# First turn of a two-layer mixer kernel: the order of its loads, and conditioning chunks taken in pairs

## The chip, the cores and the metric

The kernel runs on one core of one Trainium2 chip. The metric is the device time of one execution in microseconds; the time before is the median of 3 executions. The profile is of one execution, and its times count from the first instruction.

## The reference, cut to what matters

Two layers, each with D = 2048, a sequence of S = 256, and float32 data:

```python
mod = silu(c) @ w_ada + b_ada                 # w_ada: 2048 x 6144, one row of c
shift, scale, gate = split(mod, 3)
h = rmsnorm(x, norm_pre) * (1 + scale) + shift
z = h @ w_in                                  # w_in: 2048 x 14336, split into conv and retention parts
...                                           # short convolution, retention, group norm, gates
o = concat(y_conv, y_ret) @ w_out             # 4096 x 2048
x = x + gate * rmsnorm(o, norm_post)
```

The first layer's `h` needs the scale and the shift of every one of its 2048 rows of K, and for these all of `w_ada`'s first 4096 columns: 32 MB, before the last row group of `h` can be multiplied.

## The kernel before

**Units of work.** A weight chunk `n` is 512 columns of `w_in` or `w_out` by 2 or 4 tiles of K (0.5 or 1 MB). ScalarE rounds it (`cast`, line 586, w_hi), VectorE takes the rest (`low`, line 798, w_lo), and TensorE forms three products for each K tile and each of the two token tiles (`products`, lines 1247 to 1249): 12 matmuls for a chunk of 2 tiles, 24 for one of 4.

**The first turn** (chunks 0 to 34) goes by five K groups of 2, 2, 4, 4 and 4 tiles (`FRONT_GROUPS`), and in each group over the same seven column blocks, so that work can begin before all of the conditioning is there. Group g's chunks are 7g to 7g+6. Chunks 0 to 13 are 0.5 MB, later ones 1 MB. The sum of a block over the groups is kept in SBUF (`part`): VectorE adds chunk m's product to it (line 998) behind `low(m+2, 0)`, and TensorE waits for that add before it starts chunk m+2, which uses the same bank of PSUM (`z_wait`).

**Conditioning.** For each group there are two rows, k = 2g (scale) and k = 2g+1 (shift), each made of 2 or 4 conditioning chunks (k, kc) of 1 MB of `w_ada`, 32 in all. A chunk is taken either by TensorE (`front_chunk`, line 1286, 8 or 16 small matmuls in a 128x32 tiling into bank A) or by VectorE (`front_rows`, lines 940 and 943). Which, is said by `FRONT_VECTOR`. When all chunks of row k are in, VectorE brings bank A to SBUF (`front_row`), TensorE transposes it (`front_sum`, line 1299), VectorE reduces it and adds the bias (`front_mods`, lines 831 to 840), ScalarE forms h and rounds it (`h_full`, lines 601 and 607), and VectorE splits it (`front_split`, line 853). Only then may the group's first chunk be multiplied.

**Order.** Every engine works its queue in order, and the orders are written out by hand as tables over n: `FRONT_ROW` and `FRONT_SUM` say after which chunk a row is brought over and transposed, `FRONT_MOD` in which chunk's work VectorE forms its mods. `h_full` of group g stands on ScalarE at the end of chunk 7g-1, ahead of `cast(7g, 0)`; for group 2 (`FRONT_LATE`, chunk 14) it stands behind `cast(14, 0)`, with `front_split` behind `low(14, 0)` on VectorE. One queue (SyncE's) issues all large loads, in the order of `load_table`. There are two rings of 4 slots each, one for weight chunks and one for conditioning chunks, and SyncE waits in order for the slot of each load: that of weight chunk n-4 is free when its `low` is done, that of a conditioning chunk when TensorE or VectorE has taken it.

Of the kernel before, what the change touches and what calls it, by code (L numbers as in the profile page):

```python
# [14 lines left out]
ACT = mybir.ActivationFunctionType  # L15
# [6 lines left out]
NT = S // P  # L22
# [24 lines left out]
BLOCKS = 7  # L47
# [9 lines left out]
FRONT_GROUPS = ((0, 2), (2, 2), (4, 4), (8, 4), (12, 4))  # L57
# [7 lines left out]
def chunk_table():  # L65
# [7 lines left out]
    for l in range(LAYERS):  # L73
# [5 lines left out]
        for nb in range(NB):  # L79
            for w in range(OUT_CH):  # L80
# [8 lines left out]
FRONT = len(FRONT_GROUPS) * BLOCKS  # L89
# [25 lines left out]

FRONT_AFTER = [1, 1, 1, 1, 1, 1, 1] + [2, 1, 1, 1, 1, 1, 1] + [2, 1, 1, 1, 1, 1, 1] + [2, 1, 1, 1, 0, 0, 0]
FRONT_AFTER += [0] * BLOCKS
FRONT_CHUNKS = [(2 * g + part, kc) for g, (_, tiles) in enumerate(FRONT_GROUPS) for part in range(2)  # L120
                for kc in range(tiles)]
FRONT_FIRST = 2 * FRONT_GROUPS[0][1]
FRONT_BLOCKS = 2 * len(FRONT_GROUPS)


FRONT_VECTOR = {0: (), 1: (), 2: (), 3: (), 4: (1, 3), 5: (1,), 6: (3,)}

FRONT_LATE = 2 * BLOCKS
FRONT_ROW = {2: 2, 4: 3, 8: 4, 11: 5, 15: 6, 18: 7, 22: 8, 25: 9}
FRONT_SUM = {2: 2, 4: 3, 8: 4, 11: 5, 16: 6, 18: 7, 23: 8, 25: 9}
FRONT_MOD = {3: 2, 6: 3, 10: 4, 13: 5, 18: 6, 20: 7, 25: 8, 27: 9}

# [29 lines left out]
GATE_CHUNKS, GATE_SUM, GATE_AT = (0, 2, 4, 5), 6, 7  # L167


def front_after(n):  # L170

    at = FRONT_FIRST + sum(FRONT_AFTER[:n])
    return FRONT_CHUNKS[at:at + FRONT_AFTER[n]] if n < FRONT else []


def on_vector(k, kc):
    return kc in FRONT_VECTOR.get(k, (1, 3))


def front_done(k, kc):  # L180
# [10 lines left out]
def load_table():  # L191


    table = [("front", k, kc) for k, kc in FRONT_CHUNKS[:FRONT_FIRST]]
    for n, c in enumerate(CH):
        for m, at in enumerate(ADA_CHUNKS):
            if n in at:
                table.append(("ada", m, at.index(n)))
        if c.out and c.g in GATE_CHUNKS:
            table.append(("gate", NB * c.l + c.j, GATE_CHUNKS.index(c.g)))  # L200
        table.append(("w", n, 0))
        table += [("front", k, kc) for k, kc in front_after(n)]
    return table


# [19 lines left out]
def build(nc, x, c, positions, norm_pre, norm_post, w_ada, b_ada, w_in, conv_w, gn_gain, w_out,  # L225
          consts, decay, out):
    ctx = ExitStack()
    with ctx:  # L228
# [21 lines left out]
        xt = sb("xt", [P, NT, D])  # L250
# [24 lines left out]
        xsq = sb("xsq", [P, NT, 2])  # L275
# [10 lines left out]
        rows, _ = place("rows", [P, 2, D], F32, at_h)  # L286
        og, _ = place("og", [P, NT, D], F32, at_h + 4 * 2 * D)
        part, _ = place("part", [P, BLOCKS, NT, BLK], F32, at_yc)
        next_hi, _ = place("next_hi", [P, 2, 2, BLK], F32R, at_yr)
        next_lo, _ = place("next_lo", [P, 2, 2, BLK], F32R, at_yr + 4 * 4 * BLK)  # L290
# [287 lines left out]
        def _(act):  # L578
            N = nc.scalar

            def cast(n, h):
                if h == 0:
                    act.wait_ge(s_stage[slot_of(n)], STAGED["w", n, 0])
                if w_free(n, h):
                    act.wait_ge(s_pe, w_free(n, h))
                N.copy(w_bufs(n, h)[0], stage[:, slot_of(n), 2 * h:2 * h + 2, :]).then_inc(s_hi, 1)  # L586
# [23 lines left out]
            def h_full(l, k0, tiles):  # L610
                for k in range(k0, k0 + tiles, 2):
                    h_unit(l, k // 4, k % 4 // 2, None)

            def x_scaled(g):

                if g == 0:
                    act.wait_ge(s_pow, 1)
                else:
                    act.wait_ge(s_xt, COLUMN[0, g - 1, None] + 1)
                k0, tiles = FRONT_GROUPS[g]  # L620
                for i in range(NT):
                    ins = N.activation(v_sb[:, i, 0:P * tiles], xt[:, i, P * k0:P * (k0 + tiles)], ACT.Copy,
                                       scale=rs2[:, NT + i:NT + i + 1])
                ins.then_inc(s_xs, 1)
# [35 lines left out]
            for i in range(NT):  # L660
                act.dma_start(pos_i[:, i:i + 1], positions[0, i * P:(i + 1) * P].rearrange("(p o) -> p o", o=1))\
                    .then_inc(s_pos, 16)

            act.wait_ge(s_prm, 2)
            act.wait_ge(s_ones, 2)
            N.activation(c_cols[:, :, 0], prm[:, PRM_C:PRM_C + KT], ACT.Silu).then_inc(s_cs, 1)
            N.activation(c_silu[:, :], prm[:, PRM_C:PRM_C + KT], ACT.Silu).then_inc(s_cs, 1)
            act.wait_ge(s_x, 32)
            for i in range(NT):
                N.activation(part[:, 2 * i:2 * i + 2, :, :].rearrange("p a b c -> p (a b c)"), xt[:, i, :], ACT.Square,  # L670
                             accum_out=xsq[:, i, 0:1]).then_inc(s_xsq, 1)

            x_scaled(0)
            h_full(0, *FRONT_GROUPS[0])
            for n, ch in enumerate(CH):
                cast(n, 0)
                if n - SPILL < BLOCKS and n >= SPILL:

                    m = n - SPILL
# [111 lines left out]
        def _(dve):  # L791
# [3 lines left out]
            def low(n, h):  # L795
                hi, lo = w_bufs(n, h)
                dve.wait_ge(s_hi, HALVES[n] + h + 1)
                V.tensor_tensor(lo, stage[:, slot_of(n), 2 * h:2 * h + 2, :], hi.bitcast(F32), ALU.subtract)\  # L798
                    .then_inc(s_lo, 1)
# [44 lines left out]
            def h_split(l, g, half, i=None):  # L844
                k, lo = unit_tiles(half), tokens(i)
                tmp = tmp_buf(g)[:, k.start:k.stop, lo]
                k, hi = slice(4 * g + k.start, 4 * g + k.stop), slice(S + lo.start, S + lo.stop)
                unit = UNIT[l, g, half, i]
                if l:
                    dve.wait_ge(s_tmp, unit + 1)  # L850
                    V.tensor_copy(H[:, k, lo], tmp).then_inc(s_hhi, 1)
                dve.wait_ge(s_hhi, unit + 1)
                V.tensor_tensor(H[:, k, hi], tmp, H[:, k, lo].bitcast(F32), ALU.subtract).then_inc(s_h, 1)
# [74 lines left out]
            def front_rows(k, kc):  # L928

                tile, sem_, value = front_tile(k, kc)  # L930
                at, rows_ = front_rows_of(k, kc)
                sums = front_acc(k)[:, 0:P * FRONT_GROUPS[k // 2][1]]
                dve.wait_ge(sem_, value)
                first = min(FRONT_VECTOR.get(k, (1, 3)))
                if kc == first:
                    dve.wait_ge(s_sum, k - 1)
                for a in range(rows_):
                    c_a = c_silu[:, at + a:at + a + 1]
                    if (kc, a) == (first, 0):
                        ins = V.tensor_scalar(sums, tile[:, a, :], c_a, None, ALU.mult)  # L940
                    else:
                        me.wait()
                        ins = V.scalar_tensor_tensor(sums, tile[:, a, :], c_a, sums, ALU.mult, ALU.add)
                    me.then(ins)
                me.wait()
                dve.sem_inc(s_fv, 1)

            def front_row(k):

                cols = slice(0, P * FRONT_GROUPS[k // 2][1])  # L950
                dve.wait_ge(s_front, front_done(k, front_last(k)))
                if not FRONT_VECTOR.get(k, True):
                    if k > 1:
                        dve.wait_ge(s_sum, k - 1)
                    V.tensor_copy(front_acc(k)[:, cols], A[:, k % 2, cols]).then_inc(s_row, 1)
                else:
                    V.tensor_tensor(front_acc(k)[:, cols], A[:, k % 2, cols], front_acc(k)[:, cols], ALU.add)\
                        .then_inc(s_row, 1)

            def front_mods(k):  # L960
                mods(k, 0, 1 - k % 2, *FRONT_GROUPS[k // 2], A[:, k % 2, :])
                if k % 2:
                    gains(0, *FRONT_GROUPS[k // 2], k + 1)

            def front_split(g):
                k0, tiles = FRONT_GROUPS[g]
                for k in range(k0, k0 + tiles, 2):
                    h_split(0, k // 4, k % 4 // 2)
# [10 lines left out]
            front_mods(0)  # L979
            front_row(1)  # L980
            front_mods(1)
            h_split(0, 0, 0)

            ada_seen = 0
            for n, ch in enumerate(CH):
                low(n, 0)
                for m in range(BLOCKS, FRONT):
                    if n != m + SPILL:
                        continue
# [7 lines left out]
                    dst = v_sb[:, :, :] if (was.g, was.b) == (LAST_GROUP, VV) else part[:, was.b, :, :]  # L997
                    V.tensor_tensor(dst, Z[m % 2][:, :, :], part[:, was.b, :, :], ALU.add).then_inc(s_fin, 1)
                if n == FRONT_LATE:
                    front_split(ch.g)  # L1000
                if n == NEXT + 1:
                    x_end(0)
# [11 lines left out]
                if n == NEXT + 1:  # L1014
# [5 lines left out]
                    diagonal(1)  # L1020
                    for g in range(2):
                        h_split(1, g, None, 1)
                if n in FRONT_MOD:
                    front_mods(FRONT_MOD[n])
                if n in FRONT_ROW:
                    front_row(FRONT_ROW[n])
                if n < FRONT and ch.g < LAST_GROUP:
                    if ch.b == BLOCKS - 1 and n + 1 != FRONT_LATE:
                        front_split(ch.g + 1)
                for k, kc in front_after(n):  # L1030
                    if on_vector(k, kc):
                        front_rows(k, kc)
                if ch.l == 1 and not ch.out and ch.j == 0 and ch.b == QK and ch.g > 1:
# [183 lines left out]
        def _(pe):  # L1217
# [126 lines left out]
            for n, ch in enumerate(CH):  # L1344
# [11 lines left out]
                if n not in chain(*BY_TILES):  # L1356
                    z_wait(n)
                    for h in range(ch.halves):
# [6 lines left out]
                        pe.wait_ge(s_lo, HALVES[n] + h + 1)  # L1365
                        for i in range(NT):
                            products(n, h, i)
                for k, kc in front_after(n):
                    if not on_vector(k, kc):
                        front_chunk(k, kc)  # L1370
                if n < FRONT and ch.g < LAST_GROUP:
# [112 lines left out]
```

## Time and profile before

| | |
|---|---|
| time, median of 3 (lowest to highest) | 1730.48 us (1729.69 to 1733.38) |
| span of the profiled execution | 1727.3 us |
| TensorE busy, share of the span | 1686.8 us, 98% |
| weight loads, VectorE, ScalarE busy | 80%, 67%, 42% |
| read from HBM | 417.57 MB, mean 243 GB/s |
| mean rate in the first 200 us | 337 GB/s |

The page gives no time for the profiled execution beside its span; the median lies 3.2 us above that. Lengths of matmuls are modelled and overlap, so the starts are what counts. In rows, "idle before" is the time in which the engine stood still ahead of the instruction, with what released it.

### The profile page before, as it was taken

How to read it: one execution, taken by the hardware profiler on the slowest of the kernel's cores; microseconds unless marked ns; L12 is line 12 of the kernel's file. 1: busy time of each engine (PE TensorE's matmuls, PEld its weight loads, DVE VectorE, ACT ScalarE, POOL GpSimd, SP SyncE). 2: the span in 40 equal slices, each digit the busy share in tenths (PEclk: the TensorE clock that was granted, in tenths of full speed). 3: DMA queues.
4: the chain of work that ended last, by engine and by line, in shares of the span. 5: the costliest groups of instructions: out<-in, count | busy, mean ns of one | idle time of the engine just before them, and what ended most of it. 6: DMA issues, size and time to landing. Idle time of an engine off the chain costs nothing. (4 is left out here: it accounts for less than half of the span.)

```text
span 1727.3 us, 18931 instructions
## 1 busy us (share of the span) xinstructions
PE 1686.8 (98%) x7715; PEld 1375.8 (80%) x7715; DVE 1151.9 (67%) x1279; ACT 717.3 (42%) x800; POOL 52.5 (3%) x94
## 2 busy tenths in 40 slices
PE   6899999999999999999999999999999999999998
PEld 3567888888878887888878888888888888888886
DVE  2788767778677777777776456556555654577776
ACT  3344444434343443443454444444434444443432
POOL 4000000000000000000000000000000000000000
PEclk9999999999999999999999999999999999999999
DMA  9998665797788778877774665566556656668775
GB/s 342 383 381 317 210 202 194 258 304 264 248 290 286 276 251 296 318 273 278 280 250 164 197 202 196 189 197 219 192 179 201 216 188 189 209 243 301 284 281 190
DMA packets 233655, 429.25 MB, mean 249 GB/s; under 512 B 8664, under 2 KB 50024, under 8 KB 232800
## 3 DMA queue, kind: packets, MB, share of 16 engines
q1 hardware_dynamic: 225888, 408.97, 68.6%
q10 hardware_dynamic: 7680, 19.07, 4.1%
q8 instruction: 61, 1.00, 0.2%
q14 instruction: 26, 0.21, 0.0%
HBM read 417.57 MB, written 2.10 MB: 243 GB/s over the span
## 5 line engine op out<-in xcount | busy, mean ns | idle before, releaser
L798 DVE TENSOR_TENSOR w_lo<-stage,w_hi 128x1024 fp32r<-128x1024 f32 x574 | 692.2, 1223 | 488.6 <-ACT w_hi L586 486.3
L586 ACT CAST w_hi<-stage 128x1024 fp32r<-128x1024 f32 x574 | 594.7, 1051 | 950.8 <-PE Z L1249 559.9
L1247 PE MATMUL Z<-w_hi,H 128*128 128x512 f32 x1784 | 702.7, 394 | 15.3 <-DVE w_lo L798 9.9
L1249 PE MATMUL Z<-w_hi,H 128*128 128x512 f32 x1784 | 695.1, 390 | 0.0
L1248 PE MATMUL Z<-w_lo,H 128*128 128x512 f32 x1784 | 694.4, 389 | 0.0
L1247 PEld LDWEIGHTS Z<-w_hi,H 128*128 128x128 f32 x1784 | 335.0, 188 | 95.0 <-issue 13.3
L1249 PEld LDWEIGHTS Z<-w_hi,H 128*128 128x128 f32 x1784 | 334.9, 188 | 70.7
L1248 PEld LDWEIGHTS Z<-w_lo,H 128*128 128x128 f32 x1784 | 335.2, 188 | 67.6
L819 DVE SCALAR_TENSOR_TENSOR acc<-stage,c_silu,acc 128x512 f32<-128x512 f32 x240 | 180.2, 751 | 6.8
L1247 PE MATMUL Z<-w_hi,YC 128*128 128x512 f32 x256 | 102.0, 399 | 0.0
L1247 PE MATMUL Z<-w_hi,YR 128*128 128x512 f32 x256 | 100.6, 393 | 0.0
L1249 PE MATMUL Z<-w_hi,YC 128*128 128x512 f32 x256 | 99.7, 390 | 0.0
L1249 PE MATMUL Z<-w_hi,YR 128*128 128x512 f32 x256 | 99.7, 389 | 0.0
L1248 PE MATMUL Z<-w_lo,YC 128*128 128x512 f32 x256 | 99.7, 389 | 0.0
L1248 PE MATMUL Z<-w_lo,YR 128*128 128x512 f32 x256 | 99.6, 389 | 0.0
L1248 PEld LDWEIGHTS Z<-w_lo,YC 128*128 128x128 f32 x256 | 48.1, 188 | 11.3 <-issue 1.4
L1247 PEld LDWEIGHTS Z<-w_hi,YC 128*128 128x128 f32 x256 | 48.1, 188 | 11.3 <-issue 1.4
L1247 PEld LDWEIGHTS Z<-w_hi,YR 128*128 128x128 f32 x256 | 48.1, 188 | 10.7 <-DVE w_lo L798 0.6
L1248 PEld LDWEIGHTS Z<-w_lo,YR 128*128 128x128 f32 x256 | 48.1, 188 | 10.2 <-issue 0.2
L1249 PEld LDWEIGHTS Z<-w_hi,YR 128*128 128x128 f32 x256 | 48.1, 188 | 10.1
L1249 PEld LDWEIGHTS Z<-w_hi,YC 128*128 128x128 f32 x256 | 48.0, 188 | 10.0
L1188 POOL MEMSET behind<- 1x512 f32 (+1 forms) x16 | 7.9, 517 | 966.2 <-DVE mv L1093 886.3
(152 smaller groups left out, 727.5 us busy)
## 6 DMA issues: line engine op xcount, KB each, us to landing
stage<-in_w_in SPq DMA_DIRECT2D x186, 1024.0 KB, 5.3
stage<-in_w_ada SPq DMA_DIRECT2D x64, 1024.0 KB, 7.4
stage<-in_w_out SPq DMA_DIRECT2D x64, 1024.0 KB, 7.4
stage<-in_w_in SPq DMA_DIRECT2D x74, 512.0 KB, 5.3
front_stage<-in_w_ada SPq DMA_DIRECT2D x32, 1024.0 KB, 11.9
behind<-R ACTq DMA_DIRECT2D x14, 448.0 KB, 3.6
taps<-in_conv_w ACTq DMA_DIRECT2D x18, 256.0 KB, 6.6
xt<-in_x SPq DMA_DIRECT2D x2, 1024.0 KB, 6.7
```

The source lines that it names most:

```text
L586: N.copy(w_bufs(n, h)[0], stage[:, slot_of(n), 2 * h:2 * h + 2, :]).then_inc(s_hi, 1)
L798: V.tensor_tensor(lo, stage[:, slot_of(n), 2 * h:2 * h + 2, :], hi.bitcast(F32), ALU.subtract)\
L819: ins = V.scalar_tensor_tensor(acc[:, :], w, c_silu[:, k:k + 1], acc[:, :], ALU.mult, ALU.add)
L1188: ins = G.memset(behind_buf(t)[0:n_back, n_back - 1, 0, :], 0.0)
L1247: T.matmul(z[:, i, :], hh, wh, start=ch.first and a == 0, stop=False)
L1248: T.matmul(z[:, i, :], hh, wl, start=False, stop=False)
L1249: ins = T.matmul(z[:, i, :], hl, wh, start=False, stop=stop)
```

## The change

Loads: the weight chunks of a group go ahead, and conditioning chunks follow in pairs. Use: the place at which an engine takes a conditioning chunk (`FRONT_USE`) is now apart from the place of its load, and TensorE takes two chunks, one behind the other, after every second weight chunk or so. VectorE keeps one chunk (kc = 1) of each of the rows 6 to 9 and gives up the other six. The places of `FRONT_ROW`, `FRONT_SUM` and `FRONT_MOD` move with that. At the start, ScalarE's two squares of x come ahead of its two Silus, `cast(0, 0)` ahead of `h_full` of group 0, and VectorE's `low(0, 0)` ahead of its `h_split`. In chunk 14, `front_mods(5)` stands right ahead of `front_split`, where it stood in chunk 13.

```diff
-FRONT_AFTER = [1, 1, 1, 1, 1, 1, 1] + [2, 1, 1, 1, 1, 1, 1] + [2, 1, 1, 1, 1, 1, 1] + [2, 1, 1, 1, 0, 0, 0]
-FRONT_AFTER += [0] * BLOCKS
-FRONT_CHUNKS = [(2 * g + part, kc) for g, (_, tiles) in enumerate(FRONT_GROUPS) for part in range(2)
-                for kc in range(tiles)]
+FRONT_CHUNKS = [(2 * g + part, kc) for g in range(3) for part in range(2) for kc in range(FRONT_GROUPS[g][1])]
+FRONT_CHUNKS += [(2 * g + part, kc) for g in (3, 4) for part, kc in ((0, 0), (0, 2), (0, 1), (0, 3), (1, 0), (1, 1), (1, 2), (1, 3))]
...
-FRONT_VECTOR = {0: (), 1: (), 2: (), 3: (), 4: (1, 3), 5: (1,), 6: (3,)}
+FRONT_VECTOR = {k: (1,) if k >= 6 else () for k in range(2 * len(FRONT_GROUPS))}
...
+FRONT_LOAD = {2: 2, 4: 2, 7: 2, 9: 2, 11: 2, 12: 2, 15: 2, 16: 2, 17: 2, 18: 2, 22: 2, 23: 2, 24: 2, 25: 2}
...
+FRONT_USE = {1: ((2, 0), (2, 1)), 3: ((3, 0), (3, 1)), 6: ((4, 0), (4, 1)), 8: ((4, 2), (4, 3)),
+             10: ((5, 0), (5, 1)), 12: ((5, 2), (5, 3))}
+for g in (3, 4):
+    FRONT_USE[BLOCKS * g - 7] = ((2 * g, 0), (2 * g, 2))
+    FRONT_USE[BLOCKS * g - 5] = ((2 * g, 1), (2 * g, 3), (2 * g + 1, 0))
+    FRONT_USE[BLOCKS * g - 3] = ((2 * g + 1, 1), (2 * g + 1, 2), (2 * g + 1, 3))
 
 FRONT_LATE = 2 * BLOCKS
-FRONT_ROW = {2: 2, 4: 3, 8: 4, 11: 5, 15: 6, 18: 7, 22: 8, 25: 9}
-FRONT_SUM = {2: 2, 4: 3, 8: 4, 11: 5, 16: 6, 18: 7, 23: 8, 25: 9}
-FRONT_MOD = {3: 2, 6: 3, 10: 4, 13: 5, 18: 6, 20: 7, 25: 8, 27: 9}
+FRONT_ROW = {2: 2, 4: 3, 9: 4, 13: 5, 17: 6, 19: 7, 24: 8, 26: 9}
+FRONT_SUM = FRONT_ROW
+FRONT_MOD = {3: 2, 5: 3, 10: 4, 14: 5, 18: 6, 20: 7, 25: 8, 27: 9}
...
+            act.wait_ge(s_x, 32)
+            for i in range(NT):
+                N.activation(part[:, 2 * i:2 * i + 2, :, :].rearrange("p a b c -> p (a b c)"), xt[:, i, :], ACT.Square,
+                             accum_out=xsq[:, i, 0:1]).then_inc(s_xsq, 1)
             act.wait_ge(s_prm, 2)
...
             x_scaled(0)
+            cast(0, 0)
             h_full(0, *FRONT_GROUPS[0])
             for n, ch in enumerate(CH):
-                cast(n, 0)
+                if n:
+                    cast(n, 0)
...
             front_mods(1)
+            low(0, 0)
             h_split(0, 0, 0)
...
                 if n == FRONT_LATE:
+                    front_mods(FRONT_MOD[n])
                     front_split(ch.g)
...
-                for k, kc in front_after(n):
+                for k, kc in FRONT_USE.get(n, ()):
                     if on_vector(k, kc):
                         front_rows(k, kc)
```

TensorE's loop gets the same `FRONT_USE`, and `load_table` takes `front_loaded(n)`, which reads `FRONT_LOAD`. `on_vector` and `front_row` look `FRONT_VECTOR` up without a default.

## Rows read from the trace of the kernel before

**Rows 1.** The page: busy time of each engine, share of the span.

```profile
PE 1686.8 (98%) x7715; PEld 1375.8 (80%) x7715; DVE 1151.9 (67%) x1279; ACT 717.3 (42%) x800; POOL 52.5 (3%) x94
```

**Rows 2.** Windows by stage, whole core.

```profile
core 0: us, PE busy (x) PEld busy (x) DVE busy (x) ACT busy (x) POOL busy (x), PEclk, DMA share, GB/s
28.50:52.30 23.80, 23.71 (x152) 15.64 (x152) 10.53 (x13) 9.71 (x11) 8.93 (x15) 1.00 1.07 374
...
98.00:114.00 16.00, 14.43 (x73) 10.54 (x75) 15.57 (x17) 5.15 (x6) 0.00 (x0) 1.00 1.05 387
...
131.00:160.00 29.00, 29.00 (x144) 21.38 (x143) 25.29 (x31) 14.63 (x18) 0.00 (x0) 1.00 1.02 371
```

**Rows 3.** Waits of TensorE from 28 to 170 us: total, times, longest.

```profile
PE Z L1247 <- DVE w_lo L798: 6.0, 5, 1.8
PE Z L1247 <- DVE part L998: 3.0, 3, 1.4
PE Z L1247 <- DVE H L853: 2.2, 1, 2.2
```

**Rows 4.** Timeline, ScalarE: casts that waited for a load (chunks 2, 5, 13).

```profile
31.81 1.05 ACT L586 CAST w_hi<-stage 128x1024 fp32r<-128x1024 f32 x1 [2.92 <-DMA stage<-in_w_in]
...
46.81 1.05 ACT L586 CAST w_hi<-stage 128x1024 fp32r<-128x1024 f32 x1 [2.78 <-DMA stage<-in_w_in]
...
82.08 1.05 ACT L586 CAST w_hi<-stage 128x1024 fp32r<-128x1024 f32 x1 [2.98 <-DMA stage<-in_w_in]
```

**Rows 5.** Timeline, all engines: from row 9's transposes to chunk 28.

```profile
170.91 0.60 PE L1299 MATMUL A<-ident,acc 128*128 128x128 f32 x4
...
173.38 0.68 DVE L831 TENSOR_REDUCE c_sum<-A 128x4 f32<-128x512 f32 x1
...
174.49 1.02 ACT L601 ACTIVATE R<-B,mod,ga 128x256 f32<-128x256 f32 x2 [2.33 <-DVE ga L840]
...
177.64 1.99 ACT L586 CAST w_hi<-stage 128x1024 fp32r<-128x1024 f32 x2
...
179.86 1.22 DVE L998 TENSOR_TENSOR part<-Z,part 128x1024 f32<-128x1024 f32 x1
...
182.27 0.39 PE L1247 MATMUL Z<-w_hi,H 128*128 128x512 f32 x1
```

**Rows 6.** Timeline, TensorE: single conditioning chunks between products.

```profile
72.66 0.39 PE L1249 MATMUL Z<-w_hi,H 128*128 128x512 f32 x1
...
73.97 0.50 PE L1247 MATMUL Z<-w_hi,H 128*128 128x512 f32 x1
...
89.16 1.06 PE L1286 MATMUL A<-front_stage,c_cols 128*32 128x512 f32 x8
...
89.62 0.61 PE L1286 MATMUL A<-front_stage,c_cols 128*32 128x512 f32 x4
```

**Rows 7.** Timeline, TensorE: start and last product of chunks 24 and 25.

```profile
159.89 0.47 PE L1247 MATMUL Z<-w_hi,H 128*128 128x512 f32 x1
...
170.67 0.39 PE L1249 MATMUL Z<-w_hi,H 128*128 128x512 f32 x1
...
171.26 0.48 PE L1247 MATMUL Z<-w_hi,H 128*128 128x512 f32 x1
```

**Rows 8.** Timeline, TensorE and ScalarE: how chunk 14 started.

```profile
89.99 1.00 ACT L601 ACTIVATE R<-B,mod,ga 128x256 f32<-128x256 f32 x2
...
92.47 0.47 PE L1247 MATMUL Z<-w_hi,H 128*128 128x512 f32 x1 [2.24 <-DVE H L853]
```

**Rows 9.** Groups by line, 28.5 to 170 us: VectorE's conditioning chunks.

```profile
L943 DVE SCALAR_TENSOR_TENSOR acc<-front_stage,c_silu,acc 128x512 f32<-128x512 f32 x34 | 25.5, 751 | 1.1
```

**Rows 10.** Timelines at the start: ScalarE, VectorE, TensorE.

```profile
7.27 1.28 ACT L666 ACT_TABLE_LOAD   x1 [7.27 <-issue]
...
27.18 1.23 DVE L798 TENSOR_TENSOR w_lo<-stage,w_hi 128x1024 fp32r<-128x1024 f32 x1 [0.26 <-ACT w_hi L586]
...
28.55 0.47 PE L1247 MATMUL Z<-w_hi,H 128*128 128x512 f32 x1 [1.46 <-DVE w_lo L798]
```

More of the change, by code:

```diff
@@ L167, with front_loaded @@
 GATE_CHUNKS, GATE_SUM, GATE_AT = (0, 2, 4, 5), 6, 7
-def front_after(n):
-    at = FRONT_FIRST + sum(FRONT_AFTER[:n])
-    return FRONT_CHUNKS[at:at + FRONT_AFTER[n]] if n < FRONT else []
+def front_loaded(n):
+    at = FRONT_FIRST + sum(count for m, count in FRONT_LOAD.items() if m < n)
+    return FRONT_CHUNKS[at:at + FRONT_LOAD.get(n, 0)]
 def on_vector(k, kc):
-    return kc in FRONT_VECTOR.get(k, (1, 3))
+    return kc in FRONT_VECTOR[k]
 def front_done(k, kc):
@@ L201, in load_table @@
         table.append(("w", n, 0))
-        table += [("front", k, kc) for k, kc in front_after(n)]
+        table += [("front", k, kc) for k, kc in front_loaded(n)]
     return table
@@ L667, in _ @@
             N.activation(c_silu[:, :], prm[:, PRM_C:PRM_C + KT], ACT.Silu).then_inc(s_cs, 1)
[L668 to L671, printed above, removed]
             x_scaled(0)
+            cast(0, 0)
             h_full(0, *FRONT_GROUPS[0])
             for n, ch in enumerate(CH):
-                cast(n, 0)
+                if n:
+                    cast(n, 0)
                 if n - SPILL < BLOCKS and n >= SPILL:
@@ L933, in front_rows @@
                 dve.wait_ge(sem_, value)
-                first = min(FRONT_VECTOR.get(k, (1, 3)))
+                first = min(FRONT_VECTOR[k])
                 if kc == first:
@@ L951, in front_row @@
                 dve.wait_ge(s_front, front_done(k, front_last(k)))
-                if not FRONT_VECTOR.get(k, True):
+                if not FRONT_VECTOR[k]:
                     if k > 1:
@@ L985, in _ @@
             for n, ch in enumerate(CH):
-                low(n, 0)
+                if n:
+                    low(n, 0)
                 for m in range(BLOCKS, FRONT):
@@ L1022, in _ @@
                         h_split(1, g, None, 1)
-                if n in FRONT_MOD:
+                if n in FRONT_MOD and n != FRONT_LATE:
                     front_mods(FRONT_MOD[n])
@@ L1367, in _ @@
                             products(n, h, i)
-                for k, kc in front_after(n):
+                for k, kc in FRONT_USE.get(n, ()):
                     if not on_vector(k, kc):
```

## The prediction

> **What bounds the kernel now.** I read the page first: TensorE is busy for 98% of the span [rows 1], so the end moves only by what TensorE waits or works more or less. The windows then split the first turn. Up to 114 us the loads run at 374 to 387 GB/s, a DMA share over 1, and TensorE has gaps; from 114 us it has none, while VectorE is nearly full to 131 us and busy 25.3 of the 29.0 us after that [rows 2]. TensorE's granted clock is 1.00 in all of these stages [rows 2]. The waits say what the gaps are: 11.2 us in nine waits [rows 3], of which 1.46 us stand ahead of the first product, at 28.55 us [rows 10], so 9.7 us lie later. The largest, 2.2 us, is for h of group 2, ahead of chunk 14 [rows 3, 8]. All that this change can win is in these waits; whatever it adds to TensorE's queue behind them costs its full length. I take the kernel in two pieces, up to chunk 14 and from there to chunk 28. Behind chunk 28 nothing changes, and TensorE's lead or lag is carried to the end.
>
> **Loads up to chunk 14.** 1 MB at 387 GB/s takes 2.71 us. Before `cast(13)`, which had to wait for its data until 82.08 us [rows 4], 27.25 MB were asked for: x 2, conditioning 18, weights 7, decay 0.25. In the new order there are 16 conditioning chunks ahead of chunk 13: 25.25 MB, so it lands at 82.08 - 2 x 2.71 = 76.7 us. I checked SyncE's queue for new stalls: (5,0) needs the slot of (4,0), taken behind chunk 6 at about 54 us, when 3 MB are still under way; (6,0) needs that of (5,0), free at about 71 us, with 4 MB under way. The stream does not run dry.
>
> From `cast(13, 0)` to the end of the add behind `low(13, 0)` it is 3.44 us by the same sequence at chunk 28 (cast at 177.64, add ending at 179.86 + 1.22 = 181.08) [rows 5]. That gives 80.1 us, and chunk 13 starts at 80.2. TensorE could be there at 77.8: (3,1) is 12.75 MB into the stream, which between chunk 2 (9.5 MB, 31.81 us) and chunk 5 (14.25 MB, 46.81 us) [rows 4] is 42.1 us; then come 1.1 us for that chunk, nine products of 2.75 us (a matmul each 0.2294 us, 47 steps in 10.78 us [rows 7]), four pairs at 2.08 (below) and an estimated 1.5 us of transposes. So a shift of up to 2.3 us in the earlier work changes nothing. In this slack lie all edits of the start. `low(0, 0)` ahead of `h_split` can bring the first product forward by at most 28.55 - 27.18 = 1.4 us [rows 10]. A second activation table load between Square and Silu, of which the trace has only one, hidden, 1.28 us long [rows 10], would delay the first conditioning by about that. I take both as nothing, 0 to 0.5 us if they should meet other slips.
>
> Chunk 13 takes 2.85 us: row 5's transposes start at 83.0. From the start of such transposes to VectorE's reduce it is 0.63 us (0.60 and a hand-over), from the reduce to ScalarE's first activation 174.49 - 173.38 = 1.11 us [rows 5], from there to the product 92.47 - 89.99 = 2.48 us [rows 8]. Sum: **chunk 14 starts at 87.2 us, 5.3 us ahead** of its 92.47.
>
> **Work from chunk 14 to 28.** Before, 182.27 - 92.47 = 89.8 us [rows 5, 8]. What changes:
>
> Waits that go: of the 3.0 us for VectorE's adds [rows 3], the two behind chunk 14 hold 1.6 us. They came of `front_rows` standing in VectorE's queue; VectorE loses six conditioning chunks of four operations of 0.75 us [rows 9], 18 us of queue, and from 114 us on this was not on TensorE's path. -1.6.
>
> Conditioning on TensorE: six single chunks become six pairs. A single one costs from the last product's start, 72.66, to the next product, 73.97, 1.31 us in place of a step of 0.23, and 0.11 more because the first step behind it is longer: 1.19 us [rows 6]. Its second round of four matmuls starts 0.46 us behind the first (89.62 against 89.16) [rows 6], so a second chunk adds about two rounds, 0.89 us, and a pair costs 2.08; the bound above is 2 x 1.19 = 2.38, the one below 4 x 0.43 + 0.1 = 1.84. I take 2.08, as the row shows 0.3 us at the ends that a pair pays once. +6 x 2.08 - 6 x 1.19 = +5.3 (bounds +3.9 and +7.1).
>
> A rule bears on this. The row has 0.3 us per change between the 128x32 and the 128x128 tiling [rows 6]. The Trainium skill, page "TensorEngine Tiling (Array Packing)", section "Tiling Modes", says that changing the mode drains TensorE, and changing only the tile does not. By it a pair saves one of two drains, as I took it; without it the sum would be 1.8 us higher.
>
> New waits at chunks 21 and 28. This is the step that speaks against the change. Row 7's transposes stood behind chunk 18 and row 9's behind chunk 25, each with two products of 5.5 us ahead of the group that needs them. Now they stand behind chunks 19 and 26: one product is left, 0.35 us of transposes (171.26 - 170.91) plus 5.51 us [rows 7], 5.86 us of cover. The chain that must fit under it: 0.63 us to the reduce, then 181.08 - 173.38 = 7.70 us [rows 5] through mods, gains, two h units of two tiles each on ScalarE, `cast` of the group's first chunk (which stands behind `h_full` in ScalarE's queue), `low`, and the add ahead of that bank's use; 0.06 us to the product. That is 8.39 us, so TensorE stands still for 2.5 us, twice. Before, the reduce came 1.8 us later than the transposes allowed, and the chain still fitted. VectorE and ScalarE have nothing else in that stretch: their casts are released by products two half-chunks back. +5.1.
>
> Loads here: (7,0) needs the slot of (6,0), taken only behind chunk 14, and the stream may run dry for 1 to 2 us; but chunk 19's weights are needed 5 us after they would land, and (9,3) is needed 8 us after. 0.
>
> Sum: 89.8 - 1.6 + 5.3 + 5.1 = 98.6 us, so chunk 28 starts at 87.2 + 98.6 = 185.8, **3.5 us behind** its 182.27. A span of 1727.3 + 3.5 = 1730.8 us, and with the median lying 3.2 us above the profiled span, 1734.0 us.
>
> **Rivals.**
> 1. Chunk 13's data come earlier (no loss): the place is the stream's order up to 76.7 us, the price 1 us for each, up to the 2.3 us at which TensorE itself is the limit. Against it, `cast(13)` waited for its data with every queue full. Already 0.1 us decides that the loss stays under 0.2%; in full, +1.2 us: 1731.7.
> 2. The chain at chunks 21 and 28 is covered: it would have to be 5.86 us long in place of 8.39. Nothing in the rows shortens it; 3.5 - 5.1 = -1.6: 1728.9.
> 3. A pair costs two full chunks (2.38): +1.8, so +5.3: 1735.8. For it: no pair of 512-column chunks stands in the trace.
> 4. SyncE, waiting for a conditioning slot, holds back weights, and chunk 14 starts 2 to 3 us later: 1736.5. For it: pairs free their slots in bursts. Against: 3 to 4 MB under way.
> 5. Rivals 1 and 2 together, with the start's 1.4 us showing: -5: 1725.5.
>
> **How the numbers follow.** About 0.2%, 3.5 us, is what a measurement of this kernel can tell from no change. My forecast, +2.9 to +5, has 0.42, and a fifth of that is under the bound; rival 1 has 0.22, rival 2 0.10, rival 3 0.12, rival 4 0.08, rival 5 0.06. Slower: 0.34 + 0.12 + 0.08 = 0.54; same: 0.08 + 0.22 + 0.10 = 0.40; faster: 0.06. The likeliest case alone gives 1733.4 to 1735.5. The range must reach from half of rival 2 to rival 4: 1730.0 to 1737.0.
>
> **What would show it.** Right: the waits of TensorE up to 80 us sum to 3 to 5 us instead of nearly 10; chunk 13 waits for an add; chunk 14 starts at 87 us; pairs from start to next product take 2.1 to 2.2 us; two new waits of 2.5 us for VectorE's line 998 or 798 at about 134 and 183 us; chunk 28 starts at 186 us. Wrong: chunks 21 and 28 start without a wait, or chunk 14 starts above 89 or below 86 us, or waits come up behind chunk 28, which I hold to be shifted as a whole.

## The result, and the profile after

The changed kernel takes 1737.34 us (median of 6, 1734.82 to 1741.97) against 1728.99 us for the kernel before in the same comparison (6 runs): a ratio of 1.0044, 95% interval 1.0034 to 1.0053, or 7.6 us slower (the two medians alone lie 8.35 us apart). I had forecast slower with a chance of 0.54, and 3.5 us. The direction was right, and the 3.5 us were half of what came. The median lies just above my range of 1730 to 1737; 1728.99 us times the ratio, 1736.6, lies just inside it.

The page of the changed kernel (span 1733.8 us), against [rows 1]:

```profile
PE 1695.2 (98%) x7763; PEld 1382.4 (80%) x7763; DVE 1135.7 (66%) x1255; ACT 718.4 (41%) x801; POOL 51.8 (3%) x94
```

The waits of TensorE from 28 to 170 us (total, times, longest), which answer to [rows 3]; line 1011 is the add that was line 998, and the "issue" is the wait for h of group 2, ahead of chunk 14:

```profile
PE Z L1261 <- DVE part L1011: 4.2, 2, 2.3
PE Z L1261 <- issue: 3.7, 1, 3.7
PE A L1300 <- DMA front_stage<-in_w_ada: 0.8, 1, 0.8
```

And those from 170 to 200 us, where the kernel before had none:

```profile
PE Z L1261 <- DVE part L1011: 2.3, 1, 2.3
```

So waits up to 170 us fell from 11.2 to 8.7 us; without the 1.46 us ahead of the first product, which now starts at 26.87 us and ahead of this window, from 9.7 to 8.7. A new one of 2.34 us stands at chunk 28 as one does at chunk 21. The waits at chunks 13, 21 and 28 are those that I forecast, and the 3.65 us ahead of chunk 14 are in my sum for its start, though I did not name them. Up to 80 us they are 0.84 and 1.85, 2.7 us, a little under the 3 to 5 that I gave as a sign. What I did not forecast is in the windows by stage (PEclk is the granted clock, a mean over the window):

```profile
core 0: us, PE busy (x) PEld busy (x) DVE busy (x) ACT busy (x) POOL busy (x), PEclk, DMA share, GB/s
...
80.00:84.50 4.50, 4.48 (x13) 3.52 (x14) 2.92 (x3) 1.81 (x3) 0.00 (x0) 0.62 1.05 387
88.00:94.50 6.50, 5.78 (x14) 4.57 (x15) 4.97 (x6) 4.90 (x9) 0.79 (x2) 0.50 1.05 387
...
130.00:150.00 20.00, 17.66 (x87) 12.91 (x86) 14.79 (x18) 10.31 (x14) 0.00 (x0) 1.00 0.82 291
189.00:198.00 9.00, 8.71 (x31) 7.07 (x32) 7.32 (x8) 2.78 (x3) 0.00 (x0) 0.81 0.71 227
```

TensorE's clock was 1.00, 2.4 GHz, in all the stages of [rows 2]. Here it was granted 0.62 of it from 80 to 84.5 us, 0.50 (1.2 GHz) from 88 to 94.5 and 0.81 from 189 to 198. The timeline of TensorE in these places:

```profile
76.24 1.06 PE L1300 MATMUL A<-front_stage,c_cols 128*32 128x512 f32 x8
...
80.02 0.50 PE L1261 MATMUL Z<-w_hi,H 128*128 128x512 f32 x1 [1.85 <-DVE part L1011]
...
84.18 0.44 PE L1263 MATMUL Z<-w_hi,H 128*128 128x512 f32 x1
84.46 0.60 PE L1313 MATMUL A<-ident,acc 128*128 128x128 f32 x4
88.72 0.77 PE L1261 MATMUL Z<-w_hi,H 128*128 128x512 f32 x1 [3.65 <-issue]
...
96.77 0.39 PE L1263 MATMUL Z<-w_hi,H 128*128 128x512 f32 x1
97.09 1.92 PE L1300 MATMUL A<-front_stage,c_cols 128*32 128x512 f32 x16
98.94 0.50 PE L1261 MATMUL Z<-w_hi,H 128*128 128x512 f32 x1
...
189.29 0.50 PE L1261 MATMUL Z<-w_hi,H 128*128 128x512 f32 x1 [2.34 <-DVE part L1011]
```

Chunk 13, 12 products, starts at 80.02 us as forecast (80.2), but its last product starts 4.16 us later and not 2.6. Chunk 14 starts at 88.72; its 24 products take 8.05 us from the first start to the last, where 6.1 are usual for this chunk (6.08 in the kernel before). A pair takes 98.94 - 96.77 = 2.17 us from the last product to the next, against 1.31 for a single chunk [rows 6]. Chunk 28 starts at 189.29 us, 7.0 us behind [rows 5]; at 1.2 GHz for a part of it, it and the next four take 28.7 us where 27.1 are usual. With its first transposes for the retention heads (`turned`, at 209.47 us in the kernel before) the changed kernel is 8.77 us behind. I use the lag at this place to compare the runs below. It is read from one execution of each, and it is not carried whole to the end: in the changed kernel it has shrunk to 6.5 us at the end of the span. Between 430 and 970 us TensorE's waits for `low` (line 798, now 809) came to 3.9 us in the profile before, 2.1 in this one and 5.4 in that of e3 below, so a lag and a ratio can differ by 2 us.

The chain ahead of chunk 28, in all engines' timeline, answers to [rows 5]:

```profile
180.88 0.60 PE L1313 MATMUL A<-ident,acc 128*128 128x128 f32 x4
181.52 0.69 DVE L842 TENSOR_REDUCE c_sum<-A 128x4 f32<-128x512 f32 x1 [2.03 <-PE A L1313]
...
182.64 1.02 ACT L610 ACTIVATE R<-B,mod,ga 128x256 f32<-128x256 f32 x2 [8.07 <-DVE ga L851]
...
185.79 3.88 ACT L595 CAST w_hi<-stage 128x1024 fp32r<-128x1024 f32 x4
...
188.02 1.22 DVE L1011 TENSOR_TENSOR part<-Z,part 128x1024 f32<-128x1024 f32 x1
```

From transposes to product it is 189.29 - 180.88 = 8.41 us. I had 8.39.

At the start, the timeline of ScalarE shows a second table load between the squares and the Silus:

```profile
12.79 0.19 ACT L675 ACTIVATION_READ_ACCUMULATOR part<-xt 128x1 f32 x1
13.00 1.28 ACT L679 ACT_TABLE_LOAD   x1
14.29 0.23 ACT L679 ACTIVATE c_cols<-prm 128x16 f32<-128x16 f32 x1
```

### The profile page after: what moved, and what is told of

The parts are those of the page before. It is cut to its first block and busy times, and to the rows that moved or that the text cites. A ratio compares the mean times of both kernels' runs of the same rounds, so it can differ in the third digit from the quotient of the medians.

```text
span 1733.8 us, 18994 instructions
## 1 busy us (share of the span) xinstructions
PE 1695.2 (98%) x7763; PEld 1382.4 (80%) x7763; DVE 1135.7 (66%) x1255; ACT 718.4 (41%) x801; POOL 51.8 (3%) x94
## 5 line engine op out<-in xcount | busy, mean ns | idle before, releaser
L1261 PEld LDWEIGHTS Z<-w_hi,H 128*128 128x128 f32 x1784 | 336.2, 188 | 91.3 <-issue 11.1
```

What stands on the lines that cost most here:

```text
L1261: T.matmul(z[:, i, :], hh, wh, start=ch.first and a == 0, stop=False)
```

## The experiments

Ratios are to the kernel before, in one comparison each, with the 95% interval. "Lag" is that of the first transposes for the retention heads behind 209.47 us, in the profile.

| kernel | ratio | lag, us |
|---|---|---|
| the change | 1.0044 (1.0034 to 1.0053) | +8.8 |
| e1_sums_earlier | 0.9996 (0.9987 to 1.0006) | +0.1 |
| e2_casts_ahead | 0.9995 (0.9986 to 1.0005) | -1.0 |
| e3_late_sums_alone | 1.0036 (1.0022 to 1.0050) | +4.5 |
| e4_filled_waits | 1.0014 (1.0005 to 1.0023) | +3.4 |
| e5_silu_first | 1.0036 (1.0023 to 1.0050) | +8.3 |
| e6_ahead_vector_back | 1.0040 (1.0026 to 1.0053) | +7.2 |
| e7_loads_as_before | 1.0464 (1.0450 to 1.0478) | +79.6 |
| e8_ahead_row5_earlier | 0.9971 (0.9959 to 0.9983) | -3.4 |
| e9_all_together | 1.0007 (0.9998 to 1.0016) | +2.8 |
| e10_best | 0.9974 (0.9963 to 0.9984) | -4.0 |
| e11_two_loads_ahead | 1.0048 (1.0033 to 1.0064) | +8.0 |
| e12_one_at_a_time | 1.0053 (1.0040 to 1.0065) | +11.2 |

**e1_sums_earlier: the sums where they stood.** On the changed kernel:

```diff
-    FRONT_USE[BLOCKS * g - 3] = ((2 * g + 1, 1), (2 * g + 1, 2), (2 * g + 1, 3))
+    FRONT_USE[BLOCKS * g - 4] = ((2 * g + 1, 1), (2 * g + 1, 2), (2 * g + 1, 3))
-FRONT_ROW = {2: 2, 4: 3, 9: 4, 13: 5, 17: 6, 19: 7, 24: 8, 26: 9}
+FRONT_ROW = {2: 2, 4: 3, 9: 4, 13: 5, 17: 6, 18: 7, 24: 8, 25: 9}
```

> The changed kernel with the last three conditioning chunks of groups 3 and 4 used one weight chunk earlier (behind chunks 17 and 24) and rows 7 and 9 brought over and transposed behind chunks 18 and 25, where they stood before. Theory 1 (a chain of 8.4 us under a cover of 5.9 us makes the waits at chunks 21 and 28): both waits of 2.34 us are gone, and with the wait at chunk 28 the fall of TensorE's granted clock behind it, so 4.7 us, or up to 6.5 us with the clock, off the changed kernel's 7.6 us: 1 to 3 us above the kernel before. Rival (the waits come of something else, such as ScalarE's or VectorE's queue being late anyway): waits of about 2.3 us stay at chunks 21 and 28, and the time is that of the changed kernel, ratio about 1.004.

TensorE's waits from 28 to 210 us:

```profile
PE Z L1261 <- issue: 3.7, 1, 3.7
PE Z L1261 <- DVE part L1011: 2.0, 1, 2.0
PE A L1300 <- DMA front_stage<-in_w_ada: 0.7, 1, 0.7
```

The waits at chunks 21 and 28 are gone (what is left of line 1011 is chunk 13's), the clock stayed 1.00 behind chunk 28, and 8.3 us came off by the ratios. The rival is out. It came out better than expected; in this profile the clock did not fall in chunk 13 either, though it did at chunk 14.

**e2_casts_ahead: the same waits, removed in another way.** The sums stay late, and groups 3 and 4 take the order that group 2 has:

```diff
-FRONT_LATE = 2 * BLOCKS
+FRONT_LATE = (2 * BLOCKS, 3 * BLOCKS, 4 * BLOCKS)
...
-                if n == FRONT_LATE:
+                if n in FRONT_LATE:
                     h_full(0, *FRONT_GROUPS[ch.g])
...
-                if n == FRONT_LATE:
-                    front_mods(FRONT_MOD[n])
+                if n in FRONT_LATE:
+                    if n in FRONT_MOD:
+                        front_mods(FRONT_MOD[n])
                     front_split(ch.g)
```

> The changed kernel with groups 3 and 4 done as group 2: the first half of the group's first weight chunk is cast and lowered, and the add of two chunks back made, ahead of h (chunks 21 and 28), the sums left where the change put them. Theory 1: the part of the chain behind h (cast 1.05, low 1.23, add 1.22 us) no longer follows it, the chain from the transposes to the product is about 4.2 us and fits under 5.9 us, so both waits of 2.34 us go; again 1 to 3 us above the kernel before. Rival (the late sums themselves are the cause, wherever the cast stands): waits of over 1 us stay.

Row 7's transposes, `low(21, 0)`, the first h activation, the add and the first split, in the timeline:

```profile
129.03 0.60 PE L1314 MATMUL A<-ident,acc 128*128 128x128 f32 x4
...
130.67 1.22 DVE L809 TENSOR_TENSOR w_lo<-stage,w_hi 128x1024 fp32r<-128x1024 f32 x1
130.79 1.02 ACT L610 ACTIVATE R<-B,mod,ga 128x256 f32<-128x256 f32 x2 [1.94 <-DVE ga L851]
131.81 1.22 DVE L1011 TENSOR_TENSOR part<-Z,part 128x1024 f32<-128x1024 f32 x1
...
132.94 0.68 DVE L864 TENSOR_TENSOR H<-R,H 128x512 fp32r<-128x512 f32 x1
```

`low` and the add now run beside ScalarE's h; the first split ends at 132.94 + 0.68 = 133.6 us, 4.6 us behind the transposes' start and ahead of the end of chunk 20. Neither chunk 21 nor chunk 28 waits (the waits ahead of chunks 13 and 14 are still there), and the ratio is 0.9995. It is the length of the chain against its cover that counts, and not the place of the sums alone.

**e3_late_sums_alone: one part of the change on the kernel before.**

```diff
-FRONT_ROW = {2: 2, 4: 3, 8: 4, 11: 5, 15: 6, 18: 7, 22: 8, 25: 9}
-FRONT_SUM = {2: 2, 4: 3, 8: 4, 11: 5, 16: 6, 18: 7, 23: 8, 25: 9}
+FRONT_ROW = {2: 2, 4: 3, 8: 4, 11: 5, 15: 6, 19: 7, 22: 8, 26: 9}
+FRONT_SUM = {2: 2, 4: 3, 8: 4, 11: 5, 16: 6, 19: 7, 23: 8, 26: 9}
```

> The kernel before with one thing of the change alone: rows 7 and 9 are brought over and transposed behind chunks 19 and 26 and not 18 and 25. Theory 1: two new waits of about 2.5 us at chunks 21 and 28, 5 us or 0.3% slower than before; should TensorE's granted clock fall behind them, 1 to 3 us more. Rival (the new waits need the pairs or the new load order): no new wait, time as before.

Its waits from 28 to 210 us, against [rows 3]:

```profile
PE Z L1247 <- DVE part L998: 7.0, 6, 2.3
PE Z L1247 <- DVE w_lo L798: 5.8, 5, 1.8
PE Z L1247 <- DVE H L853: 2.1, 1, 2.1
```

Waits for the add grow from 3.0 to 7.0 us: 1.31 at chunk 21 (where a single conditioning chunk behind chunk 20 is cover), 0.39 at chunk 23 and 2.31 at chunk 28. The lag is 4.5 us, and the granted clock did not fall. The ratio says 6.2 us (3.8 to 8.7). Part of the difference is in this profile itself, where the lag has grown to 5.7 us at the end of the span. The rest may be the clock in other runs: the two fastest runs (1734.8 us, the profiled one, and 1735.0) had mean granted clocks of 0.999 and 0.998, the three slower ones (1736.4 to 1738.7 us) 0.996 and 0.997. No profile shows where theirs fell.

**e4_filled_waits: waits kept, TensorE kept busy in them.** Fillers write the half of bank A that is free there:

```diff
+WARM = {13: (5, 4), 14: (5, 8), 21: (7, 5), 28: (9, 5)}
...
             for n, ch in enumerate(CH):
+                if n in WARM:
+                    pe.wait_ge(s_mod, WARM[n][0])
+                    bridge(A[:, 0, :], WARM[n][1])
```

> The changed kernel with filler matmuls (ident by parameters into the free half of bank A, results not used) in the four waits ahead of chunks 13, 14, 21 and 28: 4, 8, 5 and 5 of them. Theory 2 (the granted clock falls to half because TensorE stands still in these waits, the longest 3.65 us): the granted clock stays 1.0 up to 200 us, chunk 13 takes 2.8 us in place of 4.4, chunk 14 5.5 and not 8, and 4 to 6 us come off: ratio 1.001 to 1.002. Rival (the falls come of the pairs, 1.9 us of small matmuls, or of the chip's power and not of these waits): the clock still falls at 81 and 89 us and the time is that of the changed kernel or 0.3 us above.

The windows of the three slow stretches of the changed kernel, here:

```profile
core 0: us, PE busy (x) PEld busy (x) DVE busy (x) ACT busy (x) POOL busy (x), PEclk, DMA share, GB/s
80.00:84.50 4.50, 4.50 (x23) 3.79 (x23) 3.69 (x6) 1.68 (x4) 0.00 (x0) 1.00 1.05 388
88.00:94.50 6.50, 6.00 (x33) 3.79 (x35) 5.84 (x6) 4.87 (x6) 0.79 (x2) 1.00 1.06 389
189.00:198.00 9.00, 9.00 (x41) 7.45 (x40) 8.83 (x8) 3.81 (x4) 0.00 (x0) 1.00 0.88 275
```

The clock is 1.00 in all of them, 5.2 us came off by the ratios and 5.4 by the lags. Chunk 14 starts at 86.88 us and chunk 28 at 185.49: my sum had 185.8, and the 98.6 us between the two are what I had added up. It is so in the other runs too: the mean granted clock is 0.997 to 0.999 in the ten of this kernel, and 0.994 or 0.995 in all six of the changed one. The pairs are all still there, so the rival that they alone bring the clock down is out. The difference between my forecast and the result is the clock.

**e11_two_loads_ahead: one pair of loads back ahead of chunk 13** (on e2's version).

```diff
-FRONT_LOAD = {2: 2, 4: 2, 7: 2, 9: 2, 11: 2, 12: 2, 15: 2, 16: 2, 17: 2, 18: 2, 22: 2, 23: 2, 24: 2, 25: 2}
+FRONT_LOAD = {2: 2, 4: 2, 7: 2, 9: 2, 11: 2, 12: 4, 16: 2, 17: 2, 18: 2, 22: 2, 23: 2, 24: 2, 25: 2}
```

> The version with casts ahead of h in groups 3 and 4, and one edit of the load order: the pair (6,0), (6,2) is loaded behind chunk 12 and not 15, so that chunk 13's weights stand 27.25 MB into the stream, as before the change. Its conditioning slots are free in time. Theory 3 (chunk 13's place in the stream sets the start of chunk 14): chunk 13's cast at 82 and not 76.5 us, chunk 14 starts at 92.3 us, 5.4 us later, ratio 1.0025 to 1.004 with the granted clock's falls in the longer waits. Rival (chunk 14 is set by the use of row 5's chunks and not by the stream): chunk 14 starts at 87 us and the ratio stays at 0.9995.

`cast(13)` on ScalarE, and the starts of chunks 13 and 14 on TensorE:

```profile
81.77 1.04 ACT L595 CAST w_hi<-stage 128x1024 fp32r<-128x1024 f32 x1 [11.18 <-DMA stage<-in_w_in]
...
85.26 0.79 PE L1262 MATMUL Z<-w_hi,H 128*128 128x512 f32 x1 [7.29 <-DVE part L1011]
...
94.75 0.77 PE L1262 MATMUL Z<-w_hi,H 128*128 128x512 f32 x1 [3.65 <-issue]
```

The cast starts at 81.77 us, 0.3 us from the kernel before [rows 4], as the bytes say, and chunk 13 5.4 us later than in e2's version. Chunk 14 is 2.4 us later than I expected and the time 9.2 us above that version's and not 5.4: the wait of 7.29 us brought the clock down for all of chunk 13 as well. So the order of loads is worth what I counted, and more when its loss becomes a wait.

**e7_loads_as_before: all loads in their old places, uses left as changed.** A failed experiment, with a use.

```diff
+FRONT_LOAD = {n: 2 if n in (7, 14, 21) else 1 for n in range(25)}
```

> The changed kernel with conditioning chunks loaded in the places where the kernel before loaded them (one behind each weight chunk, two behind chunks 7, 14 and 21); where they are used stays as changed. Theory 3 (the new order of loads is what brings chunk 14 forward, because chunk 13's weights stand 25.25 and not 27.25 MB into the stream): chunk 13's cast starts at 82 us or later in place of 76.5, chunk 14 starts at 92 us or later in place of 87 to 88.7, and the time is 4 to 8 us above the changed kernel, ratio 1.007 to 1.009. Rival (the use in pairs and not the loads' order brought chunk 14 forward): chunk 14 still starts below 90 us and the time is that of the changed kernel.

The waits of SyncE's queue up to 300 us:

```profile
SPq L547 <- PE A L1300: 112.2, 12, 22.9
SPq L547 <- DVEq L957: 51.6, 3, 18.4
```

It is 80 us slower. I had not followed the slots: with loads early and uses late, four slots are full, and SyncE, standing before a fifth conditioning load, holds back the weights behind it for 164 us in all. Loads and uses of this kernel can't be moved apart by more than the ring; e11 is the edit that separates the order from the stall.

**e6_ahead_vector_back: VectorE takes a second chunk of rows 6 to 9** (on e2's version).

```diff
-FRONT_VECTOR = {k: (1,) if k >= 6 else () for k in range(2 * len(FRONT_GROUPS))}
+FRONT_VECTOR = {k: (1, 3) if k >= 6 else () for k in range(2 * len(FRONT_GROUPS))}
```

> The version with casts ahead of h in groups 3 and 4, and VectorE given back a second chunk (kc = 3) of each of the rows 6 to 9, so that TensorE takes 8 and not 12 conditioning chunks from chunk 14 on. Theory 4 (each of these costs TensorE its full length there): two pairs at 2.05 and four singles at 1.19 us in place of six pairs, 3.4 us off, chunk 28 starts at about 178 us and the ratio is 0.997 to 0.998. Rival (VectorE's queue then makes TensorE wait for the adds of line 1011, as before the change): waits of 1 to 3 us come up from chunk 15 on, and less than 1.5 us is won.

VectorE's queue behind chunk 18, and chunk 19 on TensorE:

```profile
117.21 0.49 DVE L951 TENSOR_SCALAR acc<-front_stage,c_silu 128x512 f32<-128x512 f32 x1
117.73 2.33 DVE L954 SCALAR_TENSOR_TENSOR acc<-front_stage,c_silu,acc 128x512 f32<-128x512 f32 x3
120.27 3.11 DVE L954 SCALAR_TENSOR_TENSOR acc<-front_stage,c_silu,acc 128x512 f32<-128x512 f32 x4 [0.21 <-DVE acc L954]
123.53 1.23 DVE L809 TENSOR_TENSOR w_lo<-stage,w_hi 128x1024 fp32r<-128x1024 f32 x1
...
125.95 0.50 PE L1262 MATMUL Z<-w_hi,H 128*128 128x512 f32 x1 [3.10 <-DVE part L1011]
```

(7,1) and (7,3) follow each other for 6.2 us, and `low(19, 0)` and the add of chunk 17 stand behind them, so TensorE waits 3.1 us, and again at chunk 26. Against 3.4 us of TensorE's work saved stand 6.2 us of waits and 4.3 us of chunks 19 and 26 at a lower clock (7.0 and 8.1 us from first to last start, where 5.4 are usual): 1.0040 for 0.9995, 7.8 us slower. The rival holds. The place counts: two of VectorE's chunks in a row, 6.2 us, are longer than the weight chunk beside them; spread over two weight chunks they might fit, which was not tried.

**e12_one_at_a_time: no pairs from chunk 14 on** (on e2's version).

```diff
-    FRONT_USE[BLOCKS * g - 7] = ((2 * g, 0), (2 * g, 2))
-    FRONT_USE[BLOCKS * g - 5] = ((2 * g, 1), (2 * g, 3), (2 * g + 1, 0))
-    FRONT_USE[BLOCKS * g - 3] = ((2 * g + 1, 1), (2 * g + 1, 2), (2 * g + 1, 3))
+    for back, used in ((7, ((2 * g, 0),)), (6, ((2 * g, 2),)), (5, ((2 * g, 1), (2 * g, 3))),
+                       (4, ((2 * g + 1, 0),)), (3, ((2 * g + 1, 1), (2 * g + 1, 2))), (2, ((2 * g + 1, 3),))):
+        FRONT_USE[BLOCKS * g - back] = used
```

> The version with casts ahead of h in groups 3 and 4, with the twelve conditioning chunks of rows 6 to 9 on TensorE taken one at a time, each behind another weight chunk, in place of six pairs. If a pair saves one of two changes of tiling: each single takes 1.31 us from the last product's start to the next product, against 2.17 us for a pair, and the six pairs were worth 6 x 0.33 = 2.0 us, ratio 1.0007. Rival (a pair saves nothing): both take the same per chunk and the ratio stays at 0.9995.

The last single chunk of row 7 (behind chunk 19), the transposes that now wait for the row, and chunk 20:

```profile
130.94 0.39 PE L1264 MATMUL Z<-w_hi,H 128*128 128x512 f32 x1
131.26 1.07 PE L1301 MATMUL A<-front_stage,c_cols 128*32 128x512 f32 x8
133.14 0.66 PE L1314 MATMUL A<-ident,acc 128*128 128x128 f32 x4 [0.82 <-DVE acc L968]
...
135.41 0.80 PE L1262 MATMUL Z<-w_hi,H 128*128 128x512 f32 x1 [1.61 <-DVE part L1011]
```

Its single chunks take the expected 1.31 us where nothing stands behind them (from 124.27 to 125.59 us, for one), so two cost 2 x 1.19 = 2.38 us and a pair 2.05, as expected; what the 0.33 us at the ends consist of, no row shows. In total it is 10 us above e2's version and not 2, because (7,3) now comes right ahead of the row's copy: 0.82 us for the copy and 1.61 for the add behind it, at chunk 20 and again at chunk 27, and the clock fell four times. The price of a pair is shown by the steps, and not by the time of this kernel.

**e5_silu_first: the Silus ahead of the squares again** (on the changed kernel).

```diff
+            N.activation(c_cols[:, :, 0], prm[:, PRM_C:PRM_C + KT], ACT.Silu).then_inc(s_cs, 1)
+            N.activation(c_silu[:, :], prm[:, PRM_C:PRM_C + KT], ACT.Silu).then_inc(s_cs, 1)
             act.wait_ge(s_x, 32)
             for i in range(NT):
                 N.activation(part[:, 2 * i:2 * i + 2, :, :].rearrange("p a b c -> p (a b c)"), xt[:, i, :], ACT.Square,
...
```

> The changed kernel with ScalarE's two Silus ahead of its two squares again, as before the change. In the changed kernel's profile a second activation table load of 1.28 us stands between squares and Silu. Theory 5 (the start has slack up to chunk 13): the second table load is gone, the first conditioning chunk starts at about 12.9 us in place of 14.7, but chunk 13 still starts at 80.0 us and the time is that of the changed kernel, ratio 1.003 to 1.005. Rival (the table load is on the path): 1 to 2 us come off.

The second table load is gone, the first conditioning chunk starts at 12.48 us and not 14.66, and the first product at 26.84 against 26.87. Chunk 13 starts at 79.64 against 80.02. The interval, 1.0023 to 1.0050, overlaps the change's. The start has slack behind it, as expected.

**e8_ahead_row5_earlier and e10_best: what the experiments point to.** On e2's version, row 5 is brought over and transposed one chunk earlier:

```diff
-FRONT_ROW = {2: 2, 4: 3, 9: 4, 13: 5, 17: 6, 19: 7, 24: 8, 26: 9}
+FRONT_ROW = {2: 2, 4: 3, 9: 4, 12: 5, 17: 6, 19: 7, 24: 8, 26: 9}
-FRONT_MOD = {3: 2, 5: 3, 10: 4, 14: 5, 18: 6, 20: 7, 25: 8, 27: 9}
+FRONT_MOD = {3: 2, 5: 3, 10: 4, 13: 5, 18: 6, 20: 7, 25: 8, 27: 9}
```

> The version with casts ahead of h in groups 3 and 4, and row 5 brought over and transposed behind chunk 12 in place of 13, its mods formed in chunk 13's work. Theory 1 for group 2: the transposes fall into the wait ahead of chunk 13 and the chain of 4.2 us to chunk 14 starts 2 us earlier, so the wait of 3.65 us shrinks to about 1.5 us, the granted clock does not fall in chunk 14, and 2 to 4 us come off: ratio 0.997 to 0.9985. Rival: chunk 14 is held by its own weights or by h's place on ScalarE, and still starts at 86.9 us.

Its waits from 28 to 250 us:

```profile
PE Z L1262 <- DVE part L1011: 1.6, 1, 1.6
PE A L1314 <- DVE acc L966: 0.8, 1, 0.8
PE Z L1262 <- DVE H L864: 0.2, 1, 0.2
```

Of the 3.65 us ahead of chunk 14, 0.2 are left, and the ratio is 0.9971 (0.9959 to 0.9983): this version beats both kernels. The clock still fell once, behind the 1.61 us ahead of chunk 13. e10_best puts the Silus first and four fillers there (`WARM = {13: (5, 4)}`):

> The version with casts ahead of h in groups 3 and 4 and row 5 one chunk earlier, with the Silus first and four filler matmul pairs in the wait ahead of chunk 13. Theory 2 (the clock falls behind waits): the granted clock stays 1.0 through chunk 13, chunk 28 starts at 171.5 to 172 us, 1.5 us off that version, ratio to the kernel before 0.996. Rival (the fall does not come of the wait): clock falls at 82 us all the same and the ratio stays at 0.997.

The clock stayed 1.00 and chunk 28 starts at 172.69 + 5.5 = 178.2 us, by the same count as before, 0.6 us ahead of e8's 178.8. The lag shows 0.6 us, the ratio 0.9974 (0.9963 to 0.9984) no difference. (The expectation's 171.5 to 172 us was worked out for chunk 27, which starts at 172.69 us and in e8 at 173.28.) I expected 1.5 us; 0.89 us of waiting for the add of chunk 12 took a part of it.

**e9_all_together** had e8's edit, e6's and fillers.

> All of these together: casts ahead of h in groups 3 and 4, row 5 one chunk earlier, two chunks of rows 6 to 9 on VectorE, and three filler matmul pairs each in the waits ahead of chunks 13 and 14. If the gains add, 6 to 8 us below the kernel before, ratio 0.9955 to 0.9965. If VectorE's queue or the loads bind once TensorE is earlier, the gains do not add and the ratio is 0.997 or above.

It came to 1.0007. The gains do not add, for e6's reason: two waits of 3.1 us at chunks 19 and 26, with the clock falling behind both.

## Why the prediction was right in sign and half in size

**Loads up to chunk 14: right.** `cast(13)` at 76.5 us (76.7 forecast), chunk 13 at 80.02 (80.2). Where the clock is at 1.00 in chunk 13, chunk 14 starts at 86.9 to 87.2 us (e1, e2 and e4; forecast 87.2). The start's edits vanished in the slack, as said, although the first product came forward by 1.68 us (28.55 to 26.87), more than the 1.4 that I had called the most; only the order of the Silus was tested by itself (e5). The second table load, which I held possible, came.

**Conditioning on TensorE: right.** A pair in place of two singles: 2.17 us by start to next product, less a step of 0.23 and with 0.11 for the first step, 2.05 where I had 2.08. The row that I used was right about the ends. The rule on the drain that I quoted there from the Trainium skill, page "TensorEngine Tiling (Array Packing)", agrees with it.

**Waits that go, -1.6 us: right.** No wait stands ahead of chunks 15 and 16. The reason was put too strongly: of the six conditioning chunks that VectorE loses, three are taken ahead of chunk 14, and behind it VectorE still has four of seven.

**New waits at chunks 21 and 28: right, and now shown from three sides.** 2.34 us twice where I had 2.5 (counted from start to start, as I did, chunk 28's is 2.5), the chain 8.40 and 8.41 us (8.39). They go when the sums stand one chunk earlier (e1) and when the casts go ahead (e2), and appear in the kernel before when its sums are moved alone (e3).

**The step that was mis-sized.** It is the term of the work from chunk 14 on, with chunk 13 ahead of it: "TensorE's granted clock is 1.00 in all of these stages", read from the kernel before, was carried over to waits that it did not have. The clock fell three times behind waits of 1.85, 3.65 and 2.34 us; chunk 13 took 1.5 us more, chunk 14 1.9 and the five chunks from 28 on 1.6, together 5.0. Between the starts of chunks 14 and 28 the changed kernel takes 100.6 us where my sum had 98.6, and chunk 14 starts 1.5 us late. With fillers in the waits e4 takes 98.6 and lands 0.3 us from my sum for chunk 28. 3.4 us of work and waits (e4's lag) and 5.4 of clock are the 8.8 us of lag. None of my rivals had the clock, so it is luck and no reckoning that the range, set by other rivals, reaches as far as the result.

By ratios: 7.6 us = 2.4 (e4) + 5.2.

**A lag that is carried to the end: only roughly right.** I held the rest of the kernel to be shifted as a whole. In the spans of the profiles 8.8 us of lag became 6.5, e4's 3.4 became 2.6 and e3's 4.5 became 5.7, mostly by waits for `low` between 430 and 970 us that differ between the profiles. Whether these 0.8 to 2.3 us belong to the kernels or to the single executions, one profile of each can't tell.

## What to carry to other kernels

When a step of a hand-written order is moved by one place, write down the chain from its result to the first instruction that needs it, through every in-order queue on the way, and compare it with the work that covers it. Here an order of loads that brought chunk 14 forward by 5 us, as much as the pairs behind it cost, was turned into a loss by two sums that came one chunk late, and either of two small edits takes the loss off again (0.9996 and 0.9995); only with row 5 one chunk earlier on top of the second edit is the kernel faster than before (0.9971). A wait on TensorE costs its length and, where the clock falls behind it, something more: here 1.5 us behind 1.85, 1.9 behind 3.65 and 1.6 behind 2.34. In a sum of waits, the clock of a trace without such waits can't be taken as a constant.

## What the runs showed of the hardware that I had not expected

**The granted clock falls behind waits, but not behind all of one length.** The wait of 3.65 us ahead of chunk 14 came with 1.2 GHz in all seven profiles that had it, and so did the longer waits (7.29 us in e11, 4.6 to 11.1 us in e7) and the four of 3.1 us in e6 and e9. Of waits of 1.8 to 2.0 us ahead of chunk 13, those of the change (1.85), e5 (1.88) and e12 (1.92) were followed by a fall, and those of e1 (1.96), e2 (1.84) and e6 (1.93) were not. Of the changed kernel's two waits of 2.34 us only the second was, and the kernel before has one of 2.24 us without a fall [rows 3, 8]. The shortest with a fall behind them are 1.61 us (e8, and twice in e12, where 0.82 us of waiting stand just ahead). So below 3 us length alone does not decide, and what does stays open; the pair of small matmuls ahead of chunk 13 stands in all six of those profiles, and does not decide either. It fits that the changed kernel's six times spread over 7.2 us, and that the two with a mean clock of 0.994 are the slowest. The Trainium skill, page "TensorE: Matmul & The Clock Gate", section "HAM oscillation — how this bites in real kernels", says that waits of TensorE bring its clock down and that keeping it busy avoids this; e4's fillers, at 1.00 throughout, agree.

**One activation table serves Square after Silu, but not Silu after Square.** The kernel before has a single table load for its whole run [rows 10]; with the squares first there is a second one, 1.28 us, ahead of the Silu. The Trainium skill, page "ScalarE: Activation LUTs", section "Table sets: the hidden batching unit", says that cheap functions are in every set; it names four, and Square is not among them. It would fit with the runs that the first activation decides which set is loaded, and that the function which is in fewer sets should then come first; nothing beyond these two functions was tried. The same page of the Trainium skill, "ScalarE: Activation LUTs", section "What ACT_TABLE_LOAD costs", puts a switch at about 2.66 us with a drain; here the activation behind the load starts 1.29 us after the load's start, so the trace shows no such drain.
